# Latent attention with weighted values made feature-major, weights scaled on GpSimd, and no turns of the result

## What is computed

```python
for i in range(s // Q_BLOCK):
    q0 = i * Q_BLOCK
    kend = q0 + Q_BLOCK
    sc = (einsum("bqhd,bkhd->bhqk", q_nope[:, q0:kend], k_nope[:, :kend])
          + einsum("bqhr,bkr->bhqk", q_rope[:, q0:kend], k_rope[:, :kend]))
    sc = where(ki[None, :] <= qi[:, None], sc * scale, -inf)
    p = softmax(sc, axis=-1)
    outs.append(einsum("bhqk,bkhd->bqhd", p, v[:, :kend]))
o = concatenate(outs, axis=1)
return o.reshape(b, s, MLA_HEADS * V_DIM) @ w_out
```

## Time and profile before

| | |
|---|---|
| median of 3 runs | 1299.64 us (1299.39 to 1300.07) |
| profiled execution | 1299.49 us, its span 1297.8 us |
| TensorE clock granted, mean | 0.998 |
| TensorE busy | 98% of the span |
| VectorE, ScalarE, GpSimd busy | 59%, 53%, 9% |

### The profile page before, as it was taken

How to read it: one execution, slowest core, us unless ns; L and a number is a source line. 1 busy time by engine, 2 the same in 40 slices (tenths; PEclk the granted TensorE clock), 3 DMA queues, 4 the chain that set the end, 5 groups by cost and what they waited for, 6 DMA issues and landing times.

```text
span 1297.8 us, 18319 instructions
## 1 busy us (share of the span) xinstructions
PE 1277.3 (98%) x6934; PEld 1094.6 (84%) x6934; DVE 763.6 (59%) x892; ACT 682.2 (53%) x924; POOL 122.3 (9%) x198
## 2 busy tenths in 40 slices
PE   8999999999999999999999999989999999999997
PEld 7888889999888888888888888877888888999896
DVE  5655645878795655554555545765655554666654
ACT  6544435669883644443544534854644443444554
POOL 3000000008730000000000001620000000000000
PEclk9999999999999999999999999999999999999999
DMA  9656646453246466555655463412566565565431
GB/s 300 206 183 209 218 144 195 145 181 98 98 163 219 137 194 194 186 203 163 194 180 180 175 227 110 161 54 79 193 194 192 193 213 162 148 192 182 147 114 49
DMA packets 180653, 219.81 MB, mean 169 GB/s; under 512 B 8713, under 2 KB 132942, under 8 KB 180590
## 3 DMA queue, kind: packets, MB, share of 16 engines
q1 hardware_dynamic: 179614, 218.01, 51.8%
q10 hardware_dynamic: 688, 0.79, 0.2%
q0 software_dynamic: 288, 0.15, 0.0%
HBM read 217.87 MB, written 1.05 MB: 169 GB/s over the span
## 4 chain that ended last, share of the span: by engine, by line
PE 89%; ACT 4%; DVE 4%; issue 1%; DMA 1%; SPq 1%; POOL 1%; DVEq 0%; POOLq 0%; ACTq 0%
PE acc L622 27%; PE acc L624 27%; PE acc L623 27%; PE tr L639 4%; DVE w_lo L1974 1%; ACT w_hi L1367 1%; PE tr L933 1%; DMA raw<-in_ffn_w_up 1%; PE aux L1075 1%; PE acc L1056 1%; ACT xT_hi L1379 0%; ACT R_hi L1578 0%; ACT junk L1433 0%; SPq L510 0%; PE aux L924 0%
## 5 line engine op out<-in xcount | busy, mean ns | idle before, releaser
L1974 DVE TENSOR_TENSOR w_lo<-raw,w_hi 128x2048 fp32r<-128x2048 f32 (+2 forms) x187 | 420.4, 2275 | 176.4 <-ACT w_hi L1367 176.2
L1367 ACT ACTIVATE w_hi<-raw 128x2048 fp32r<-128x2048 f32 (+2 forms) x189 | 352.1, 1897 | 118.0 <-PE acc L624 117.2
L622 PE MATMUL acc<-w_hi,xT_hi 128*128 128x512 f32 (+1 forms) x914 | 362.4, 396 | 0.7 <-DVE w_lo L2594 0.4
L624 PE MATMUL acc<-w_hi,xT_lo 128*128 128x512 f32 (+1 forms) x914 | 355.1, 388 | 0.0
L623 PE MATMUL acc<-w_lo,xT_hi 128*128 128x512 f32 (+1 forms) x914 | 354.2, 388 | 0.0
L624 PEld LDWEIGHTS acc<-w_hi,xT_lo 128*128 128x128 f32 x914 | 171.6, 188 | 36.2
L622 PEld LDWEIGHTS acc<-w_hi,xT_hi 128*128 128x128 f32 x914 | 171.8, 188 | 35.8 <-issue 1.6
L623 PEld LDWEIGHTS acc<-w_lo,xT_hi 128*128 128x128 f32 x914 | 172.0, 188 | 33.0
L622 PE MATMUL acc<-w_hi,hT_hi 128*128 128x512 f32 x448 | 176.0, 393 | 0.4 <-DVE y_sb L2494 0.4
L624 PE MATMUL acc<-w_hi,hT_lo 128*128 128x512 f32 x448 | 174.5, 389 | 0.0
L623 PE MATMUL acc<-w_lo,hT_hi 128*128 128x512 f32 x448 | 174.4, 389 | 0.0
(11 more groups left out here) (298 smaller groups left out, 1160.4 us busy)
## 6 DMA issues: line engine op xcount, KB each, us to landing
raw<-in_ffn_w_down SPq DMA_DIRECT2D x88, 512.0 KB, 4.9
raw<-in_ffn_w_gate SPq DMA_DIRECT2D x86, 512.0 KB, 4.2
raw<-in_ffn_w_up SPq DMA_DIRECT2D x86, 512.0 KB, 5.2
raw<-in_ssm_w_in SPq DMA_DIRECT2D x48, 512.0 KB, 4.6
raw<-in_w_in_a SPq DMA_DIRECT2D x64, 256.0 KB, 4.1
raw<-in_ssm_w_out SPq DMA_DIRECT2D x16, 512.0 KB, 4.0
raw<-in_mla_w_out SPq DMA_DIRECT2D x8, 512.0 KB, 4.4
raw<-in_w_out_a SPq DMA_DIRECT2D x8, 512.0 KB, 5.0
```

The lines of the kernel that those rows point to most:

```text
L622: pe.matmul(o, lh, rh, start=start, stop=False, skip_group_check=skip)
L624: return pe.matmul(o, ll, rh, start=False, stop=stop, skip_group_check=skip)
L1367: inst = act.activation(w_hi[:, u % RING, 0:n], raw[:, u % RING, 0:n], ACT.Copy)
L1974: inst = dve.tensor_tensor(w_lo[:, u % RING, 0:n], raw[:, u % RING, 0:n], w_hi[:, u % RING, 0:n].bitcast(F32), ALU.subtract)
```

## The change

The values become the stationary operand (64 columns, one head) and the turned weights the moving one (128 columns), so the result comes out with features on the partitions: even heads in rows 0 to 63, odd heads in rows 64 to 127 of `aux`. The product with the reciprocal can't be made there for each query, since queries now lie along the free axis; it is made on the weights, before their turn: `exps` sums each row beside the Exp, VectorE takes the reciprocal (`scale_weights`), and GpSimd multiplies `pm` in place (128x512) and signals `p_scaled`, for which `weights_turn` waits. `out_norm`, `out_turn`, `o_tok` and the column of ones go; `out_high` and `out_low` read `aux` itself, once a round.

```diff
                 def weights_turn(r):
-                    p, b = round_bank(r)
-                    acc_done(pe, p0 + p, b)
+                    pe.wait_ge(p_scaled, r + 1)
                     turn([(j * P, pm[:, r % 3, j * P:(j + 1) * P]) for j in range(4)], k0 + MLA_TURNS["t", r])
...
-                    for j in range(nh):
+                    for pair in range(nh // 2):
                         for kb in range(tb + 1):
-                            at = (j * (tb + 1) + kb) * P
-                            last = pe.matmul(aux[:, r % 2, j * (VD + 1):(j + 1) * (VD + 1)], pT[:, r % 2, at:at + P],
-                                             kv_tok[:, kb, h0 + j, NOPE:], start=kb == 0, stop=kb == tb)
+                            for j in (2 * pair, 2 * pair + 1):
+                                at = (j * (tb + 1) + kb) * P
+                                last = pe.matmul(aux[j % 2 * VD:(j % 2 + 1) * VD, r % 2, pair * P:(pair + 1) * P],
+                                                 kv_tok[:, kb, h0 + j, NOPE:], pT[:, r % 2, at:at + P],
+                                                 start=kb == 0, stop=kb == tb, skip_group_check=True)
                     last.then_inc(o_ready, 1)
...
-                    turn_done(pe, k0 + MLA_TURNS["o", 4 * tb + n])
+                    pe.wait_ge(o_read, 4 + k + 1 if tb else n + 1)
...
                         inst = act.activation(pm[:, r % 3, j * w:(j + 1) * w], bank(p0 + p, b)[:, j * w:(j + 1) * w],
-                                              ACT.Exp, bias=nbias[:, tb, h0 + j:h0 + j + 1])
+                                              ACT.Exp, bias=nbias[:, tb, h0 + j:h0 + j + 1],
+                                              accum_out=psums[:, tb, h0 + j:h0 + j + 1])
...
+                def out_high(r):
+                    act.wait_ge(o_ready, r + 1)
+                    if r < 4:
+                        inst = act.activation(xT_hi[:, 2 * r:2 * r + 2, 0:P], heads(aux[:, r % 2, 0:2 * P], 2), ACT.Copy)
+                    else:
+                        inst = act.activation(xT_hi[:, r - 4, P:T], aux[:, r % 2, 0:P], ACT.Copy)
+                    inst.then_inc(turn_hi, 1)
...
+                def scale_weights(r):
                     tb, h0, nh = mla_round(r)
...
+                    p, b = round_bank(r)
+                    acc_done(dve, p0 + p, b)
+                    pi = pinv[:, tb, h0:h0 + nh]
+                    dve.reciprocal(pi, psums[:, tb, h0:h0 + nh]).then_inc(p_inverse, 1)
...
+                    dve.tensor_tensor(xT_lo[at], o, xT_hi[at].bitcast(F32), ALU.subtract).then_inc(o_read, 1)
...
+                for r in range(ROUNDS):
+                    tb, h0, nh = mla_round(r)
+                    pool.wait_ge(p_inverse, r + 1)
+                    v = heads(pm[:, r % 3, :], nh)
+                    pool.tensor_tensor(v, v, pinv[:, tb, h0:h0 + nh].unsqueeze(2).to_broadcast([P, nh, P * (tb + 1)]),
+                                       ALU.mult).then_inc(p_scaled, 1)
```

TensorE's order of the rest is kept, without the `out_turn` calls. ScalarE's queue from Exp 0 on becomes: exps 0, 1, 2, read_weights 0, 2, out_high 0, keys, exps 3, out_high 1, keys, out_high 2, exps 4, 5, out_high 3, read_weights 4, exps 6, split of u0+10, out_high 4, exps 7, split of u0+11, out_high 5, read_weights 6, exps 8, out_high 6, and so on. VectorE's queue:

```diff
-                for r in range(4):
+                for r in range(3):
                     tops(r)
+                scale_weights(0)
+                tops(3)
+                scale_weights(1)
+                scale_weights(2)
                 read_weights(1)
-                out_norm(0)
-                out_norm(1)
+                out_low(0)
                 read_turn("k", 1, 1)
-                out_low(0)
+                out_low(1)
+                scale_weights(3)
                 read_turn("k", 1, 3)
-                out_norm(2)
+                out_low(2)
                 tops(4)
                 read_weights(3)
                 tops(5)
-                out_low(1)
-                out_norm(3)
-                out_low(2)
+                scale_weights(4)
+                out_low(3)
                 split_to(u0 + 10)
                 tops(6)
-                out_low(3)
-                out_norm(4)
+                scale_weights(5)
+                out_low(4)
                 split_half(u0 + 10, 0)
                 read_weights(5)
+                tops(7)
                 split_half(u0 + 10, 1)
-                tops(7)
-                out_norm(5)
+                scale_weights(6)
+                out_low(5)
+                tops(8)
+                scale_weights(7)
                 split_half(u0 + 11, 0)
-                tops(8)
-                split_half(u0 + 11, 1)
-                out_low(4)
-                out_norm(6)
+                out_low(6)
                 read_weights(7)
                 tops(9)
-                out_norm(7)
+                scale_weights(8)
+                split_half(u0 + 11, 1)
+                out_low(7)
                 tops(10)
-                out_low(5)
-                out_norm(8)
+                scale_weights(9)
+                out_low(8)
                 read_weights(9)
                 tops(11)
-                out_norm(9)
+                scale_weights(10)
+                out_low(9)
+                scale_weights(11)
```

More of the change, by code:

```diff
@@ L159 @@
     + [("k", 0, quad) for quad in range(4)]
[3 rows of a table removed]
+    + [("t", 0), ("t", 1), ("t", 2), ("k", 1, 0), ("k", 1, 1), ("k", 1, 2), ("k", 1, 3)]
+    + [("t", r) for r in range(3, 12)])}
 def mamba_slots(n, sums_first=False):
@@ L390, in program @@
         o_read = sem("o_read")
+        p_inverse = sem("p_inverse")
+        p_scaled = sem("p_scaled")
         first_half = sem("first_half")
@@ L1128, in mla @@
                 scores(6)
-                out_turn(3)
                 values(4)
@@ L1750, in read_weights @@
                     turn_free(act.activation(pT[:, r % 2, :], tr[:, k % 2, :], ACT.Copy), k)
-                def out_high(n):
-                    tb, m = n // 4, n % 4
-                    k = k0 + MLA_TURNS["o", n]
-                    act.wait_ge(turned, k + 1)
-                    act.activation(xT_hi[:, 2 * m:2 * m + 2, tb * P:(tb + 1) * P], heads(tr[:, k % 2, 0:2 * P], 2),
-                                   ACT.Copy).then_inc(turn_hi, 1)
+                def out_high(r):
[5 more added lines that the diff above has]
+                    inst.then_inc(turn_hi, 1)
                 read_proj(0, 0)
@@ L1800, in mla @@
                 exps(1)
+                exps(2)
                 read_weights(0)
-                exps(2)
                 read_weights(2)
+                out_high(0)
                 read_turn("k", 1, 0)
                 exps(3)
-                out_high(0)
+                out_high(1)
                 read_turn("k", 1, 2)
+                out_high(2)
                 exps(4)
-                out_high(1)
                 exps(5)
-                out_high(2)
+                out_high(3)
                 read_weights(4)
                 exps(6)
-                out_high(3)
                 split_to(u0 + 11)
+                out_high(4)
                 exps(7)
                 split_to(u0 + 12)
+                out_high(5)
                 read_weights(6)
                 exps(8)
-                out_high(4)
+                out_high(6)
                 exps(9)
+                out_high(7)
                 read_weights(8)
                 exps(10)
-                out_high(5)
+                out_high(8)
                 exps(11)
+                out_high(9)
                 read_weights(10)
-                out_high(6)
+                out_high(10)
                 split_to(u0 + 13)
-                out_high(7)
+                out_high(11)
                 c.unit, c.pair, c.turn = u0 + 12, p0 + 21, k0 + len(MLA_TURNS)
@@ L2368, in read_weights, with out_low @@
                     turn_free(dve.tensor_copy(pT[:, r % 2, :], tr[:, k % 2, :]), k)
-                def out_norm(r):
+                def scale_weights(r):
                     tb, h0, nh = mla_round(r)
-                    dve.wait_ge(o_ready, r + 1)
-                    o = heads(aux[:, r % 2, 0:nh * (VD + 1)], nh)
-                    pi = pinv[:, tb, h0:h0 + nh].unsqueeze(2)
-                    link(dve.reciprocal(pi, o[:, :, VD:]))
-                    dve.tensor_tensor(heads(o_tok[:, tb, h0 * VD:(h0 + nh) * VD], nh), o[:, :, 0:VD],
-                                      pi.to_broadcast([P, nh, VD]), ALU.mult).then_inc(o_read, 1)
-                def out_low(n):
-                    tb, m = n // 4, n % 4
-                    k = k0 + MLA_TURNS["o", n]
+                    p, b = round_bank(r)
+                    acc_done(dve, p0 + p, b)
+                    pi = pinv[:, tb, h0:h0 + nh]
+                    dve.reciprocal(pi, psums[:, tb, h0:h0 + nh]).then_inc(p_inverse, 1)
+                def out_low(r):
                     c.high += 1
                     dve.wait_ge(turn_hi, c.high)
-                    at = (slice(None), slice(2 * m, 2 * m + 2), slice(tb * P, (tb + 1) * P))
-                    turn_free(dve.tensor_tensor(xT_lo[at], heads(tr[:, k % 2, 0:2 * P], 2), xT_hi[at].bitcast(F32),
-                                                ALU.subtract), k)
+                    if r < 4:
```

(4 more changed lines are left out.)

28 lines of the change are left out of this document (6 added, 22 removed), and 3 rows, old and new, of the table MLA_TURNS.

## The result

| | kernel before | changed kernel |
|---|---|---|
| median (lowest to highest), 12 executions each | 1299.16 us (1298.55 to 1300.07) | 1302.51 us (1300.85 to 1304.64) |
| ratio | | 1.0026 (95%: 1.0019 to 1.0034) |
| profiled execution, span | 1299.49 us, 1297.8 | 1303.36 us, 1301.5 |
| granted clock, mean | 0.998 | 0.996 |

The change makes the kernel 3.35 us slower. The forecast was 1301.2 us, 1.6 over its base; the interval lies inside the range. The median is on the side of "slower by over 0.2%", which had a chance of 0.33, though the interval reaches down to 1.0019. The loss is twice the 1.6 us that were forecast.

What follows compares the result with a forecast made beforehand. TensorE, busy 98% of the span, was taken as the bound; 3.7 us of removed work was expected to be given back in waits, net +1.6 us, 1301.2. Range 1295.5 to 1304.8; the forecast's own 1299.2 to 1302.8.

Steps and rivals of the forecast that it cites:

- What goes and what the values cost: TensorE in the rounds: eight result turns go, 1.76 us; value rounds take 0.65 us, saving 1.9 us over 12 rounds.
- The chain: From scores to weight turn: sums, reciprocal and GpSimd's product make the turn 1.3 to 1.6 us later after the last Exp.
- The start: 857 to 869 us: the first product with the output weights starts at 868.5 instead of 868.95, 0.45 us early.
- The middle: 869 to 899 us: VectorE's queue order delays TensorE; the second half's products start 2.0 us late.
- The step called the surest: Last unit's second half split comes after round 9's top and round 8's reciprocal; TensorE waits 1.4 us.
- The sum: Whole kernel: +1.6 us on the profiled 1299.49 is 1301.1, as a median 1301.2.
- rival (4): TensorE's clock falls to its lower level after waits in the start, two microseconds of work taking four: 1303.2; 5%.
- Rival (1): Rounds: waits only change place and the removed TensorE work shows in full, -3.7 us, 1295.9; 22%.
- Rival (2): GpSimd's product costs 1.35 us or more beside VectorE and goes first at the last unit's split: +3.9, 1303.5; 20%.
- Rival (3): Value rounds: column halves do not overlap with 128 columns, +0.43 us in about eight rounds, 1304.6; 7%.

Runs made afterwards that it cites:

- head by head: Changed kernel with each pair's value products in rounds 4 to 11 issued one head after the other instead of by turns: 1301.70 us, ratio 1.0017.
- the other order: ScalarE's and VectorE's splits moved earlier and last waits on TensorE filled with due work, in both kernels: kernel before 1297.62 us, changed kernel 1294.38 us.

## Why the prediction was right

- **What goes and what the values cost.** The turns are gone; the value round takes 0.59 us, forecast 0.65. Right, by a row of the same form elsewhere in the trace.
- **The chain.** Exp with its sum 0.34 us from start to start (855.59 to 855.93), forecast 0.37; reciprocal 0.15 to 0.18; GpSimd 1.04, forecast 1.06; beside a split 1.94. Right.
- **The start.** With the 0.48 us from before the rounds taken off, the first turn of weights stands at 858.19 (forecast 858.15), the wait before round 3's turn is 1.08 us (1.25), and the first product with the output weights starts at 868.54 (868.5).
- **The middle.** Marks with 0.48 taken off, forecast in brackets: third unit 880.6 (880.75), turn of round 7 886.5 (886.8), last unit 890.1 (890.3) after 1.39 us of waiting (1.4), turn of round 10 898.8 (898.7) after 1.38 (1.3), turn of round 11 finished 901.5 (901.15; 0.36 us of it are the lower clock, 0.77 us for a turn that took 0.41 head by head). The step called the surest, the half split behind a top, was confirmed by moving it alone.
- **The sum.** Rounds and remainder came to +1.7 (2.0 - 0.3), forecast +1.6, and the second measurement of the same work (head by head) is 2.1 us over the kernel before. What failed in size is the clock, rival (4): it was given 5% and priced in the start, because the waits there are short, and the sum has it at nothing. In the profiled execution it fell after 900 us, behind two waits of 1.38 and 0.69 us, and cost 1.5 us. With the 0.5 us from before the rounds the profile comes to +3.7 and the median to +3.35, so the outcome is "slower" rather than "within 0.2%". That the median still lies in the forecast's own range, 1299.2 to 1302.8, is owed to the width of that range and not to the sum.
- **Rival (1)**, the removed work in full: wrong for this order, true to within 0.5 us when both kernels have the other order. **Rival (2)**, GpSimd over 1.3 us or first at the split: wrong; ten of the twelve products took 1.04 us, and VectorE was first at the other two. That the product matters was right: without it 2.7 us go. **Rival (3)**: wrong, with the right price.

The 0.5 us before the rounds are not the change's. The turn of `q_tok` at 837 us waits 1.04 to 1.07 us for VectorE in the profiles of the changed kernel, of the head-by-head run and of the kernel before with sums and in another order, 0.4 us in the others. The rows of VectorE and GpSimd ahead of it, first of the kernel before, then of the changed kernel:

```profile
832.75 0.18 DVE L2326 TENSOR_SCALAR newton<-newton 128x32 f32<-128x32 f32 x1
832.75 1.34 POOL L2770 TENSOR_TENSOR t<-q_tok,rope_a 128x512 f32<-128x512 f32 x1
832.97 1.17 DVE L2327 TENSOR_TENSOR qrs<-qrs,newton 128x32 f32<-128x32 f32 x1
...
832.59 1.30 POOL L2765 TENSOR_TENSOR t<-q_tok,rope_a 128x512 f32<-128x512 f32 x1
832.60 1.33 DVE L2319 TENSOR_SCALAR newton<-newton 128x32 f32<-128x32 f32 x1
833.96 0.68 DVE L2320 TENSOR_TENSOR qrs<-qrs,newton 128x32 f32<-128x32 f32 x1
```

Two short steps of VectorE meet one product of GpSimd that starts at the same moment to 0.01 us. Where the first step gets in ahead it takes 0.18 us and only the second one is held up; where GpSimd gets in ahead, the first step takes 1.33 us, and VectorE begins `q_tok` 0.5 us later (834.68 instead of 834.17). All four late profiles have the row of 1.32 to 1.33 us, the other ten that of 0.18, and both kinds occur in variants of both kernels. How often it goes either way in the executions without a profile is not known.

What stays open: which waits let the clock fall. The same waits left it up in one profile and were followed by the lower clock in another, twice.

## What to carry to other kernels

An engine that is busy half of the time can be the bound by its order: walk the queue from the last thing that each call waits for, and ask of every call behind it who needs it first. When a wait is removed by moving one call, look for the second releaser that arrives just as late. When one profile is set against another, look first for a profile of the same work: here two of them differ by 1.6 us in the rounds, by the clock. When work is taken from the bounding engine, plan its queue partners anew; here the same edit cost 3.35 us in the order it came with, and brought 3.2 against a kernel before whose queues had been arranged as well.

## What the runs showed of the hardware

- After a wait of 1.38 us and one of 0.69 us, the waiting products 1.3 us apart, TensorE's clock fell from 2.4 to 1.2 GHz, into 904 to 906 us, and 9.56 us of work took 11.03. With the same two waits it stayed at 1.00 in the head-by-head run. Waits of 0.9 and 1.07 us were followed by the lower clock in the run without the product and not in the changed kernel.
- Two narrow float32 products on different column halves overlap even when the queue holds them head by head; on one half the round takes 1.02 instead of 0.59 us.
- GpSimd's product beside a half split of VectorE took 1.94 instead of 1.04 us and the split lost nothing, because the split had started 0.16 us earlier. In the earlier trace rows a split lost 0.8 us (3.12 instead of 2.28): it started at 296.66, when GpSimd was still at two products that end at 297.64, so here too the one that had started first went first:

```profile
294.70 2.94 POOL L2691 TENSOR_TENSOR R_lo<-upto,dA_lo 128x512 fp32r<-128x512 f32 x2
```

- Who starts first can hang on 0.01 us: a VectorE step of 0.18 us took 1.33 when a GpSimd product of 1.30 us had got in ahead of it, and this moved the rest of the kernel by about 0.5 us.
